# First attention's steps in the order scores, turn, values, turn, and the perceptron's opening units and sums in another order

## The chip, the cores and the metric

The kernel runs on one core of one Trainium2 chip. The metric is device time in microseconds (us), the median of several runs. The core has TensorE for matmuls and transposes, VectorE, ScalarE and GpSimd for the rest, and SyncE, which issues the transfers. Each engine takes its own list of instructions in the order in which the program writes it, and engines meet at semaphores.

## The reference

Two blocks run one after the other on 256 tokens of width 1024, all in float32. What bears on this change is the first layer of the first block:

```
h = h + ab_layer(rms_norm(h, attn_norm[0]))          # two mixers of 8 heads each, then w_out
h = h + square(relu(rms_norm(h, mlp_norm[0]) @ w1)) @ w2   # w1 1024 x 4096, w2 4096 x 1024

fox_mixer, per head:  p = softmax(q k^T / 8 + cum_q - cum_k, causal);   o = p v
dsa_mixer, per head:  p = softmax(latent scores, over the 64 keys picked per query);   o = p v
```

The second layer has another attention (16 heads) and a second perceptron of the same form. The second block, attention again in four steps and a projection, is not touched.

## The kernel before, in words

Weights come as 270 units of 128 x 1024 numbers. ScalarE rounds a unit to its high part (L458), VectorE subtracts to get the low part (L463), and TensorE multiplies high by high, high by low and low by high; this pair of instructions is called a split. The order of everything is written out by hand.

**First attention.** Eight steps, numbered 0 to 7, have two heads each; steps 0 to 3 are the mixer with decay, 4 to 7 the one with picked keys. A step passes through these stages:

- *scores* on TensorE (`ab_scores`, L999, for steps 0 to 3 with L994 before it);
- *peaks* on VectorE (`ab_peaks`, L2000): four passes that add the mask, store the scores in `probs` and find the rows' maxima. `probs` has three slots, so the peaks of a step wait until both turns of the step three before it are through (`s_turned`);
- *exponentials* on ScalarE (L1481), and a reciprocal on GpSimd (L1893);
- two *turns* on TensorE (`turn_p`, L974): three transposes each into the one PSUM bank `ptp`, the first turn for head 0, the second for head 1;
- after each turn a copy out of `ptp`: the first by ScalarE (`p_first`, L1469), the second by VectorE (`p_second`, L2030). A turn waits (`s_copied`) until the copy of the turn before it is done, since the bank is one;
- *values* on TensorE (`mix`, L444): twelve matmuls of 64 columns into `misc`;
- a scaling on VectorE (`ab_scaled`, L2036) into `o_tok`.

Iteration `it` handles the scores and peaks of step `it`, the exponentials of step `it - 1`, the turns and copies of step `it - 3`, and the values and scaling of step `it - 4`. `ab_iter` sets the order on TensorE; a loop at the end of the part for VectorE and one in the part for ScalarE set theirs. In some iterations they also split the first three units of the output projection, and in iterations 8 and 9 blocks of `o_tok` are turned (L408) and copied (L473, L488).

**Perceptron.** `mlp` is called twice, once per layer. Its first two hidden units of 128 need no loop: per unit eight *wide* matmuls (L815, 512 columns: high weights by both parts of x) and eight *narrow* ones (L822, 256 columns: low weights by the high part). The first unit sums in `ptp`, the second in `misc`. Between them stand the turns of the last four column blocks of h (L408), which wait for VectorE's sum into h (L1991). When a unit's narrow ones are done, ScalarE copies half of the bank (`cross`, L1501), VectorE adds it to the other half (`up_sum`, first instruction, L2062) and squares (L2067), ScalarE rounds (`high`, L1507) and VectorE subtracts (`low`, L2072). The wide matmuls of hidden unit 2 use the first bank again and wait for unit 0's L2062; those of unit 3 wait for unit 1's.

Of the kernel before, what the change touches and what calls it, by code (L numbers as in the profile page):

```python
# [60 lines left out]
LEAD = 3  # L61
# [143 lines left out]
def program(nc, x, stream, consts_d, cols_d, rows_d, sel_d, out):  # L205
    with ExitStack() as ctx:  # L206
# [470 lines left out]

        STEPS_AB = A_HEADS // 2 + B_HEADS // 2
        FOX = B_HEADS // 2
        STEPS_C = C_HEADS  # L680
        CO_SPLITS = (5, 8, 14)

# [91 lines left out]
        def _(pe):  # L774
# [25 lines left out]
            def turn_h(b, h0, cc):  # L800

                pe.wait_ge(h_done, h0 + 2 * (cc // 2) + 2)
                pe_turn_block(pe, b, h, (cc,))

            def mlp(f0, u0, b, h0, next_b, next_h0):
                def up_wide(f, u, i=None, blocks_k=range(KD)):

                    if blocks_k[0] == 0:
                        pe.wait_ge(w_lo, at(u + 1, i, UPS))
                    if blocks_k[0] == 0 and f0 + f >= 2:  # L810
                        pe.wait_ge(z_summed, at(f0 + f - 1, i, TPP))
                    for k in blocks_k:
                        if f == 0 and k % 2 == 0:
                            pe.wait_ge(lo_out, 4 * b + k // 2 + 1)
                        nc.tensor.matmul((ptp, misc)[f % 2][:, :], wh[:, u % SPLIT, k * P:(k + 1) * P],  # L815
                                         xhl[:, KD + k, :, :].rearrange("p a s -> p (a s)"),
                                         start=k == 0, stop=False, skip_group_check=True)

                def up_narrow(f, u, blocks_k=range(KD)):

                    for k in blocks_k:
                        last = nc.tensor.matmul((ptp, misc)[f % 2][:, 0:SEQ], wl[:, u % SPLIT, k * P:(k + 1) * P],  # L822
                                                xh[:, KD + k, :], start=False, stop=k == KD - 1,
                                                skip_group_check=True)
                    if blocks_k[-1] == KD - 1:
                        last.then_inc(w_used, 1)

                def down_part(f, u, half, tiles=range(T), opens=False):

                    ws = slice(half * 512, (half + 1) * 512)  # L830
                    for t in tiles:
                        ts = slice(t * P, (t + 1) * P)
                        last = mm3(acc[2 * half + t][:, :], hh[:, f % 2, ts], hl[:, f % 2, ts],
                                   wh[:, u % SPLIT, ws], wl[:, u % SPLIT, ws], opens, f == FT - 1)
                    return last

                def down_ready(f, u, i=None):
                    pe.wait_ge(w_lo, at(u + 1, i, UPS))
                    pe.wait_ge(hid_lo, at(f0 + f + 1, i, TPP))

                def down(f, u, i=None):

                    down_ready(f, u, i)
                    down_part(f, u, 0, opens=f == 0)
                    down_part(f, u, 1, opens=f == 0).then_inc(w_used, 1)

                up_wide(0, u0, blocks_k=range(4))
                turn_h(b, h0, 2)
                turn_h(b, h0, 3)
                up_wide(1, u0 + 1, blocks_k=range(4))  # L850
                up_narrow(0, u0, range(4))
                up_narrow(1, u0 + 1, range(4))
                for ks in (range(4, 6), range(6, KD)):
                    up_wide(0, u0, blocks_k=ks)
                    up_wide(1, u0 + 1, blocks_k=ks)
                up_narrow(0, u0, range(4, KD))
                up_narrow(1, u0 + 1, range(4, KD))

                def two_tiles(f, i=None):

                    u = u0 + 2 + 2 * f
                    up_wide(f + 2, u, i)
                    up_wide(f + 3, u + 1, i)
                    up_narrow(f + 2, u)
                    up_narrow(f + 3, u + 1)
                    down(f, u + 2, i)
                    down(f + 1, u + 3, i)

                for f in range(0, TPP, 2):
                    two_tiles(f)  # L870
                with pe.Fori(0, PASSES - 1) as i:
                    for f in range(TPP, 2 * TPP, 2):
                        two_tiles(f, i)
                u = u0 + 2 * FT - 2
                down_ready(FT - 2, u)
                down_part(FT - 2, u, 0)
                down_ready(FT - 1, u + 1)
                down_part(FT - 1, u + 1, 0).then_inc(half_summed, 1)
                down_part(FT - 2, u, 1).then_inc(w_used, 1)
                down_part(FT - 1, u + 1, 1, (0,))  # L880
                turn_h(next_b, next_h0, 0)
                down_part(FT - 1, u + 1, 1, (1,)).then_inc(w_used, 1)
                turn_h(next_b, next_h0, 1)
# [126 lines left out]

            def ab_iter(it):

                if 0 <= it - DEEP < STEPS_AB:
                    turn_p(it - DEEP, 0)
                if it < STEPS_AB:
                    ab_scores(it)
                if it >= STEPS_AB:
                    mix(it - DEEP - 1, ab_values(it - DEEP - 1))
                if 0 <= it - DEEP < STEPS_AB:
                    turn_p(it - DEEP, 1)  # L1020
                if DEEP < it < STEPS_AB:
                    if it == DEEP + 1:
                        pe.wait_ge(ev_act, left(G_ABO))
                        pe.wait_ge(ev_dve, left(G_ABO))
                    mix(it - DEEP - 1, ab_values(it - DEEP - 1))

            def between(u):

# [422 lines left out]
        def _(act):  # L1451
# [43 lines left out]
            def mlp(f0, u0, n, next_b, next_gain):  # L1495
                def cross(f, u_end, i=None):

                    act.wait_ge(w_used, at(u_end, i, UPS))
                    if f0 + f >= 2:
                        act.wait_ge(z_summed, at(f0 + f - 1, i, TPP))  # L1500
                    s_.activation(probs[:, f % 2, 0:SEQ], (ptp, misc)[f % 2][:, SEQ:2 * SEQ],  # L1501
                                  ACT.Copy).then_inc(z_cross, 1)

                def high(f, u_free, i=None):
                    act.wait_ge(sqr_done, at(f0 + f + 1, i, TPP))
                    act.wait_ge(w_used, at(u_free, i, UPS))
                    s_.activation(hh[:, f % 2, :], hq[:, f % 2, :], ACT.Copy).then_inc(hid_hi, 1)  # L1507

                split(u0 + LEAD)
                cross(0, u0 + 1)  # L1510
                split(u0 + 1 + LEAD)
                cross(1, u0 + 2)
                high(0, u0)
                high(1, u0)
                act_sumsq(act, n)
                with act.Fori(0, PASSES) as i:
                    for f in range(0, TPP, 2):
                        u = u0 + 2 + 2 * f
                        split(u + LEAD, i)
                        cross(f + 2, u + 1, i)  # L1520
                        split(u + 1 + LEAD, i)
                        cross(f + 3, u + 2, i)
                        split(u + 2 + LEAD, i)
                        high(f + 2, u + 3, i)
                        split(u + 3 + LEAD, i)
                        high(f + 3, u + 4, i)
                u = u0 + 2 * FT - 2
                split(u + LEAD)
                act_turn_block(act, next_b, next_gain, (0, 1))
                split(u + 1 + LEAD)  # L1530
# [91 lines left out]
            for it in range(1, STEPS_AB + DEEP):  # L1622
                if 0 <= it - DEEP < STEPS_AB:
                    p_first(it - DEEP)
                if it - 1 < STEPS_AB:
                    exponentials(it - 1)
                if 0 <= it - (STEPS_AB - 3) < LEAD:
                    split(U_ABO + it - (STEPS_AB - 3))
                if it in (STEPS_AB, STEPS_AB + 1):
                    act_turn_block(act, 1, ccs=(it - STEPS_AB,))  # L1630
                if it == 1:
# [338 lines left out]
        def _(dve):  # L1970
# [84 lines left out]
            def mlp(f0, u0, next_b, next_gain):  # L2055
# [18 lines left out]

                split(u0 + LEAD)
                up_sum(0)
                split(u0 + 1 + LEAD)
                low(0)
                up_sum(1)
                low(1)  # L2080
                with dve.Fori(0, PASSES) as i:
                    for f in range(0, TPP, 2):
# [150 lines left out]
                scaled(st, o_tok[:, :, 2 * HD * st:2 * HD * (st + 1)].rearrange("p t (a d) -> p a t d", a=2), rs)  # L2233

            for it in range(STEPS_AB + DEEP):
                if 0 <= it - DEEP < STEPS_AB:
                    p_second(it - DEEP)
                if it < STEPS_AB - 1:
                    ab_peaks(it)
                if it > DEEP:  # L2240
                    ab_scaled(it - DEEP - 1)
                if it == STEPS_AB - 1:
                    ab_peaks(it)
                if 0 <= it - (STEPS_AB - 2) < LEAD:
                    split(U_ABO + it - (STEPS_AB - 2))
                if it in (STEPS_AB, STEPS_AB + 1):
                    dve_turn_block(dve, 1, ccs=(it - STEPS_AB,))
                if it == 0:
# [445 lines left out]
```

## Time and profile before

| what | value |
|---|---|
| median of 3 runs | 907.81 us (907.81 to 908.78) |
| the profiled execution, its own time | 908.62 us |
| its span, first to last instruction | 906.8 us |
| TensorE busy | 890.7 us, 98% of the span |
| VectorE busy | 645.2 us |
| ScalarE busy | 510.1 us |
| mean granted TensorE clock | 0.998 |
| first attention's last turn begins | 115.85 us |

A share near 98% says that time is lost only where TensorE stands still or runs at a lower clock, so the places where it waits are read one by one in its timeline. In a timeline row the first number is the start, the second the duration; square brackets hold the idle time before it and the engine that ended it. Durations of TensorE's instructions overlap, so distances between starts are the better measure.

### The profile page before, as it was taken

How to read it: one execution, taken by the hardware profiler on the slowest of the kernel's cores; microseconds unless marked ns; L12 is line 12 of the kernel's file. 1: busy time of each engine (PE TensorE's matmuls, PEld its weight loads, DVE VectorE, ACT ScalarE, POOL GpSimd, SP SyncE). 2: the span in 40 equal slices, each digit the busy share in tenths (PEclk: the TensorE clock that was granted, in tenths of full speed). 3: DMA queues.
4: the chain of work that ended last, by engine and by line, in shares of the span. 5: the costliest groups of instructions: out<-in, count | busy, mean ns of one | idle time of the engine just before them, and what ended most of it. 6: DMA issues, size and time to landing. Idle time of an engine off the chain costs nothing. (4 is left out here: it accounts for less than half of the span.)

```text
span 906.8 us, 14857 instructions
## 1 busy us (share of the span) xinstructions
PE 890.7 (98%) x4796; PEld 745.2 (82%) x4796; DVE 645.2 (71%) x1305; ACT 510.1 (56%) x1017; POOL 124.5 (14%) x168
## 2 busy tenths in 40 slices
PE   8999999999999999999999999999999999999998
PEld 7878787888888888888878888888887778878876
DVE  4768756766666679687467666666876878777775
ACT  6654835444454466586354454444656666666573
POOL 1310300000000000354010000000430401400401
PEclk9999999999999999999999999999999999999999
DMA  9643143655555557010436565555464445454431
GB/s 343 225 158 98 46 144 123 210 198 191 191 194 193 190 178 247 33 47 25 140 116 217 196 192 192 195 191 188 141 223 145 140 140 182 147 182 141 162 117 47
DMA packets 41609, 145.75 MB, mean 161 GB/s; under 512 B 4688, under 2 KB 6224, under 8 KB 41552
## 3 DMA queue, kind: packets, MB, share of 16 engines
q1 hardware_dynamic: 41264, 144.93, 48.4%
q8 instruction: 34, 0.56, 0.3%
q14 instruction: 23, 0.19, 0.1%
q10 hardware_dynamic: 288, 0.07, 0.0%
HBM read 143.93 MB, written 1.05 MB: 160 GB/s over the span
## 5 line engine op out<-in xcount | busy, mean ns | idle before, releaser
L463 DVE TENSOR_TENSOR wl<-raw,wh 128x1024 fp32r<-128x1024 f32 (+2 forms) x270 | 329.1, 1222 | 88.7 <-ACT wh L458 86.2
L458 ACT ACTIVATE wh<-raw 128x1024 fp32r<-128x1024 f32 (+2 forms) x270 | 281.6, 1046 | 64.9 <-PE acc L355 43.4
L353 PE MATMUL acc<-wh,xhl 128*128 128x512 f32 (+1 forms) x472 | 190.7, 404 | 0.6 <-DVE xhl L2490 0.4
L355 PE MATMUL acc<-wh,xhl 128*128 128x512 f32 (+1 forms) x472 | 184.4, 391 | 0.0
L354 PE MATMUL acc<-wl,xhl 128*128 128x512 f32 (+1 forms) x472 | 183.9, 390 | 0.0
L353 PEld LDWEIGHTS acc<-wh,xhl 128*128 128x128 f32 x472 | 88.7, 188 | 25.0 <-issue 8.0
L355 PEld LDWEIGHTS acc<-wh,xhl 128*128 128x128 f32 x472 | 88.6, 188 | 19.2
L354 PEld LDWEIGHTS acc<-wl,xhl 128*128 128x128 f32 x472 | 88.8, 188 | 16.3
L353 PE MATMUL acc<-wh,hh 128*128 128x512 f32 x256 | 100.2, 391 | 0.0
L354 PE MATMUL acc<-wl,hh 128*128 128x512 f32 x256 | 100.0, 391 | 0.0
L355 PE MATMUL acc<-wh,hl 128*128 128x512 f32 x256 | 99.6, 389 | 0.0
L1507 ACT ACTIVATE hh<-hq 128x256 fp32r<-128x256 f32 x64 | 26.7, 418 | 77.3 <-PE acc L355 72.5
L815 PE MATMUL ptp<-xhl,wh 128*128 128x512 f32 x256 | 64.1, 390 | 1.1 <-DVE hr L2062 1.1
L1501 ACT ACTIVATE probs<-ptp 128x256 f32<-128x256 f32 x32 | 12.3, 383 | 93.7 <-PE ptp L822 93.7
L815 PE MATMUL misc<-xhl,wh 128*128 128x512 f32 x256 | 64.3, 391 | 0.7 <-DVE hr L2062 0.7
L2062 DVE TENSOR_TENSOR hr<-ptp,probs 128x256 f32<-128x256 f32 x32 | 13.6, 424 | 67.5 <-ACT probs L1501 67.5
L507 POOL TENSOR_SCALAR st<-st 128x2 f32<-128x2 f32 x7 | 2.4, 338 | 430.8 <-ACT o_tok L500 258.2
L815 PEld LDWEIGHTS misc<-xhl,wh 128*128 128x128 f32 x256 | 47.8, 188 | 11.2 <-DVE wl L463 1.5
L815 PEld LDWEIGHTS ptp<-xhl,wh 128*128 128x128 f32 x256 | 47.8, 188 | 11.2 <-issue 1.4
L355 PEld LDWEIGHTS acc<-wh,hl 128*128 128x128 f32 x256 | 48.1, 188 | 10.2
L353 PEld LDWEIGHTS acc<-wh,hh 128*128 128x128 f32 x256 | 48.2, 188 | 9.3
L354 PEld LDWEIGHTS acc<-wl,hh 128*128 128x128 f32 x256 | 48.2, 188 | 8.7
(302 smaller groups left out, 1355.2 us busy)
## 6 DMA issues: line engine op xcount, KB each, us to landing
raw<-stream SPq DMA_DIRECT2D x266, 512.0 KB, 3.4
raw<-stream SPq DMA_DIRECT2D x4, 352.0 KB, 5.7
h<-x SPq DMA_DIRECT2D x4, 256.0 KB, 4.0
out<-h SPq DMA_DIRECT2D x3, 256.0 KB, 2.1
row<-rows SPq DMA_DIRECT2D x1, 700.0 KB, 8.8
probs<-sel SPq DMA_DIRECT2D x1, 512.0 KB, 7.7
cst<-consts SPq DMA_DIRECT2D x1, 507.0 KB, 7.1
out<-h SPq DMA_DIRECT2D x2, 128.0 KB, 2.0
```

Of the source, the lines that this page charges most:

```text
L353: nc.tensor.matmul(out_, ah, bh, start=start, stop=False, skip_group_check=True)
L354: nc.tensor.matmul(out_, ah, bl, start=False, stop=False, skip_group_check=True)
L355: return nc.tensor.matmul(out_, al, bh, start=False, stop=stop_, skip_group_check=True)
L458: nc.scalar.activation(used(u, wh[:, u % SPLIT, :]), used(u, raw[:, u % RAW, :]), ACT.Copy).then_inc(w_hi, 1)
L463: nc.vector.tensor_tensor(used(u, wl[:, u % SPLIT, :]), used(u, raw[:, u % RAW, :]), used(u, wh[:, u % SPLIT, :]).bitcast(F32), ALU.subtra ...
L507: chain_link(nc.gpsimd.tensor_scalar(dst, src, 1.0 / width, EPS, ALU.mult, ALU.add))
L815: nc.tensor.matmul((ptp, misc)[f % 2][:, :], wh[:, u % SPLIT, k * P:(k + 1) * P], xhl[:, KD + k, :, :].rearrange("p a s -> p (a s)"), star ...
L1501: s_.activation(probs[:, f % 2, 0:SEQ], (ptp, misc)[f % 2][:, SEQ:2 * SEQ], ACT.Copy).then_inc(z_cross, 1)
L1507: s_.activation(hh[:, f % 2, :], hq[:, f % 2, :], ACT.Copy).then_inc(hid_hi, 1)
L2062: v_.tensor_tensor(hr[:, f % 2, :], bank[:, 0:SEQ], probs[:, f % 2, 0:SEQ], ALU.add).then_inc(z_summed, 1)
```

## The change

It has four parts.

1. TensorE, first attention: iterations 4 to 7 issue scores, first turn, values, second turn. Before, they issued first turn, scores, second turn, values.
2. VectorE, first attention: an iteration issues peaks, scaling, copy of the second turn. Before: copy, peaks, scaling (in iteration 7 copy, scaling, peaks).
3. The three splits of the output projection's units stand in iterations 3, 4 and 6 on ScalarE and 4, 5 and 7 on VectorE. Before: 5, 6, 7 and 6, 7, 8.
4. Perceptron, both calls: the narrow matmuls of unit 0 stand earlier in both halves of the opening, and ScalarE and VectorE do both copies and both sums ahead of the second split.

```diff
+        ABO_SPLITS = (3, 4, 6)
...
                 up_wide(0, u0, blocks_k=range(4))
+                up_narrow(0, u0, range(4))
                 turn_h(b, h0, 2)
                 turn_h(b, h0, 3)
                 up_wide(1, u0 + 1, blocks_k=range(4))
-                up_narrow(0, u0, range(4))
                 up_narrow(1, u0 + 1, range(4))
-                for ks in (range(4, 6), range(6, KD)):
-                    up_wide(0, u0, blocks_k=ks)
-                    up_wide(1, u0 + 1, blocks_k=ks)
+                up_wide(0, u0, blocks_k=range(4, 6))
+                up_wide(1, u0 + 1, blocks_k=range(4, 6))
+                up_wide(0, u0, blocks_k=range(6, KD))
                 up_narrow(0, u0, range(4, KD))
+                up_wide(1, u0 + 1, blocks_k=range(6, KD))
                 up_narrow(1, u0 + 1, range(4, KD))
...
             def ab_iter(it):
-                if 0 <= it - DEEP < STEPS_AB:
-                    turn_p(it - DEEP, 0)
+                if it == DEEP:
+                    turn_p(0, 0)
                 if it < STEPS_AB:
                     ab_scores(it)
-                if it >= STEPS_AB:
+                if DEEP < it < STEPS_AB + DEEP:
+                    turn_p(it - DEEP, 0)
+                if it == DEEP + 1:
+                    pe.wait_ge(ev_act, left(G_ABO))
+                    pe.wait_ge(ev_dve, left(G_ABO))
+                if it > DEEP:
                     mix(it - DEEP - 1, ab_values(it - DEEP - 1))
                 if 0 <= it - DEEP < STEPS_AB:
                     turn_p(it - DEEP, 1)
-                if DEEP < it < STEPS_AB:
-                    if it == DEEP + 1:
-                        pe.wait_ge(ev_act, left(G_ABO))
-                        pe.wait_ge(ev_dve, left(G_ABO))
-                    mix(it - DEEP - 1, ab_values(it - DEEP - 1))
...
ScalarE, mlp
                 split(u0 + LEAD)
                 cross(0, u0 + 1)
+                cross(1, u0 + 2)
                 split(u0 + 1 + LEAD)
-                cross(1, u0 + 2)
                 high(0, u0)
                 high(1, u0)
...
ScalarE, first attention
-                if 0 <= it - (STEPS_AB - 3) < LEAD:
-                    split(U_ABO + it - (STEPS_AB - 3))
+                if it in ABO_SPLITS:
+                    split(U_ABO + ABO_SPLITS.index(it))
...
VectorE, mlp
                 split(u0 + LEAD)
                 up_sum(0)
+                up_sum(1)
                 split(u0 + 1 + LEAD)
                 low(0)
-                up_sum(1)
                 low(1)
...
VectorE, first attention
             for it in range(STEPS_AB + DEEP):
-                if 0 <= it - DEEP < STEPS_AB:
-                    p_second(it - DEEP)
-                if it < STEPS_AB - 1:
+                if it < STEPS_AB:
                     ab_peaks(it)
                 if it > DEEP:
                     ab_scaled(it - DEEP - 1)
-                if it == STEPS_AB - 1:
-                    ab_peaks(it)
-                if 0 <= it - (STEPS_AB - 2) < LEAD:
-                    split(U_ABO + it - (STEPS_AB - 2))
+                if 0 <= it - DEEP < STEPS_AB:
+                    p_second(it - DEEP)
+                if it - 1 in ABO_SPLITS:
+                    split(U_ABO + ABO_SPLITS.index(it - 1))
```

What stands in a row on VectorE in iteration 5 (the second turn's copy of step 2, the peaks of step 5, the scaling of step 1), each row with the semaphores it waits for. Iteration 4 has the same form but another mask. Before:

```order
L2030 COPY pt<-ptp 128x384 [waits s_mixed,s_turned]
L2000 ISA probs,nb<-pair,picked 128x128 [waits s_scored,s_turned]
L2000 ISA nb 128x1
L2000 ISA probs,nb<-pair,picked 128x256
L2000 ISA nb 128x1
L2000 ISA probs,nb<-acc,picked 128x128 [waits s_scored]
L2000 ISA nb 128x1
L2000 ISA probs,nb<-acc,picked 128x256
L2000 ISA nb 128x1
L2036 TENSOR_TENSOR o_tok<-misc,rs 128x2x2x64 [waits s_coef,s_mixed]
```

After (two or three lines further down in the file):

```order
L2003 ISA probs,nb<-pair,picked 128x128 [waits s_scored,s_turned]
L2003 ISA nb 128x1
L2003 ISA probs,nb<-pair,picked 128x256
L2003 ISA nb 128x1
L2003 ISA probs,nb<-acc,picked 128x128 [waits s_scored]
L2003 ISA nb 128x1
L2003 ISA probs,nb<-acc,picked 128x256
L2003 ISA nb 128x1
L2039 TENSOR_TENSOR o_tok<-misc,rs 128x2x2x64 [waits s_coef,s_mixed]
L2033 COPY pt<-ptp 128x384 [waits s_mixed,s_turned]
```

The copy moved from ahead of the four passes and the scaling to behind them; the passes wait for the same `s_turned` count as the copy.

TensorE from the second turn of step 0 on (L974 a turn, L999 the scores of step 4, L444 the values of step 0). Before:

```order
L974 MATMUL ptp<-cst,probs 128x128 [waits s_copied,s_exped]
L974 MATMUL ptp<-cst,probs 128x128 x2
L974 MATMUL ptp<-cst,probs 128x128 [waits s_copied,s_exped]
L974 MATMUL ptp<-cst,probs 128x128 x2
L999 MATMUL pair<-QK 128x128 [waits s_peaked]
L999 MATMUL acc<-QK 128x128
L999 MATMUL pair<-QK 128x256
L999 MATMUL acc<-QK 128x256
L974 MATMUL ptp<-cst,probs 128x128 [waits s_copied,s_exped]
L974 MATMUL ptp<-cst,probs 128x128 x2
L444 MATMUL misc<-Y,pt 128x64 [waits s_copied,ev_dve,ev_act]
L444 MATMUL misc<-Y,pt 128x64 x5
```

After:

```order
L977 MATMUL ptp<-cst,probs 128x128 [waits s_copied,s_exped]
L977 MATMUL ptp<-cst,probs 128x128 x2
L1002 MATMUL pair<-QK 128x128 [waits s_peaked]
L1002 MATMUL acc<-QK 128x128
L1002 MATMUL pair<-QK 128x256
L1002 MATMUL acc<-QK 128x256
L977 MATMUL ptp<-cst,probs 128x128 [waits s_copied,s_exped]
L977 MATMUL ptp<-cst,probs 128x128 x2
L444 MATMUL misc<-Y,pt 128x64 [waits s_copied,ev_dve,ev_act]
L444 MATMUL misc<-Y,pt 128x64 x5
L977 MATMUL ptp<-cst,probs 128x128 [waits s_copied,s_exped]
L977 MATMUL ptp<-cst,probs 128x128 x2
```

The first turn of step 1 moved behind the scores, its second turn behind the values of step 0.

TensorE in the perceptron's opening, from the last column blocks' turns on (`ptp` holds hidden unit 0, `misc` unit 1). Before:

```order
L408 MATMUL pair<-cst,h 128x128 x3
L815 MATMUL misc<-xhl,wh 128x512 [waits w_lo]
L815 MATMUL misc<-xhl,wh 128x512 x3
L822 MATMUL ptp<-xhl,wl 128x256 x4
L822 MATMUL misc<-xhl,wl 128x256 x4
L815 MATMUL ptp<-xhl,wh 128x512 [waits lo_out]
L815 MATMUL ptp<-xhl,wh 128x512
L815 MATMUL misc<-xhl,wh 128x512 x2
L815 MATMUL ptp<-xhl,wh 128x512 [waits lo_out]
L815 MATMUL ptp<-xhl,wh 128x512
L815 MATMUL misc<-xhl,wh 128x512 x2
L822 MATMUL ptp<-xhl,wl 128x256 x4
```

After:

```order
L408 MATMUL pair<-cst,h 128x128 x3
L816 MATMUL misc<-xhl,wh 128x512 [waits w_lo]
L816 MATMUL misc<-xhl,wh 128x512 x3
L823 MATMUL misc<-xhl,wl 128x256 x4
L816 MATMUL ptp<-xhl,wh 128x512 [waits lo_out]
L816 MATMUL ptp<-xhl,wh 128x512
L816 MATMUL misc<-xhl,wh 128x512 x2
L816 MATMUL ptp<-xhl,wh 128x512 [waits lo_out]
L816 MATMUL ptp<-xhl,wh 128x512
L823 MATMUL ptp<-xhl,wl 128x256 x4
L816 MATMUL misc<-xhl,wh 128x512 x2
L823 MATMUL misc<-xhl,wl 128x256 x4
```

Four narrow matmuls of unit 0 left this stretch (they now stand ahead of the turns of h), and its last four stand ahead of unit 1's last two wide ones.

## Rows read from the trace of the kernel before

**Rows 1.** The page: busy time of each engine, and the granted clock in 40 slices.
```profile
PE 890.7 (98%) x4796; PEld 745.2 (82%) x4796; DVE 645.2 (71%) x1305; ACT 510.1 (56%) x1017; POOL 124.5 (14%) x168
...
PEclk9999999999999999999999999999999999999999
```

**Rows 2.** Timeline of TensorE, first attention: start, duration, what, idle before.
```profile
94.53 0.55 PE L974 MATMUL ptp<-cst,probs 128*128 128x128 f32 x3
95.82 0.52 PE L974 MATMUL ptp<-cst,probs 128*128 128x128 f32 x3 [0.74 <-DVE pt L2030]
...
97.12 0.55 PE L974 MATMUL ptp<-cst,probs 128*128 128x128 f32 x3
97.51 1.45 PE L444 MATMUL misc<-Y,pt 128*128 128x64 f32 x12
98.79 0.50 PE L974 MATMUL ptp<-cst,probs 128*128 128x128 f32 x3
...
107.75 0.50 PE L974 MATMUL ptp<-cst,probs 128*128 128x128 f32 x3
...
111.23 0.52 PE L974 MATMUL ptp<-cst,probs 128*128 128x128 f32 x3 [0.41 <-DVE pt L2030]
...
114.16 0.52 PE L974 MATMUL ptp<-cst,probs 128*128 128x128 f32 x3 [0.30 <-DVE pt L2030]
...
115.85 0.50 PE L974 MATMUL ptp<-cst,probs 128*128 128x128 f32 x3
```

**Rows 3.** Timeline of VectorE, first attention.
```profile
95.11 0.56 DVE L2030 COPY pt<-ptp 128x384 f32<-128x384 f32 x1 [0.61 <-PE ptp L974]
...
104.09 0.28 DVE L2000 CUSTOM_DVE_ANT_0 probs<-pair,picked 128x128 f32<-128x128 f32 x1
...
105.19 0.42 DVE L2036 TENSOR_TENSOR o_tok<-misc,rs 128x256 f32<-128x256 f32 x1
105.53 1.22 DVE L463 TENSOR_TENSOR wl<-raw,wh 128x1024 fp32r<-128x1024 f32 x1
```

**Rows 4.** Timeline of TensorE, perceptron's opening and first loop units.
```profile
142.95 1.09 PE L408 MATMUL pair<-cst,h 128*128 128x128 f32 x8 [0.66 <-DVE h L1991]
...
147.60 0.64 PE L822 MATMUL ptp<-xhl,wl 128*128 128x256 f32 x4
148.07 0.64 PE L822 MATMUL misc<-xhl,wl 128*128 128x256 f32 x4
149.26 2.09 PE L815 MATMUL ptp<-xhl,wh 128*128 128x512 f32 x8 [0.55 <-DVE hr L2062]
151.68 2.08 PE L815 MATMUL misc<-xhl,wh 128*128 128x512 f32 x8 [0.32 <-DVE hr L2062]
...
160.98 1.98 PE L815 MATMUL ptp<-xhl,wh 128*128 128x512 f32 x8
162.79 1.98 PE L815 MATMUL misc<-xhl,wh 128*128 128x512 f32 x8
```

**Rows 5.** Timelines of ScalarE (first row) and VectorE, perceptron's opening.
```profile
148.28 0.39 ACT L1501 ACTIVATE probs<-ptp 128x256 f32<-128x256 f32 x1 [2.11 <-PE ptp L822]
...
144.52 1.66 DVE L491 SCALAR_TENSOR_TENSOR xhl<-pair,col,xhl 128x256 fp32r<-128x256 f32 x4 [1.62 <-ACT xhl L476]
...
148.69 0.42 DVE L2062 TENSOR_TENSOR hr<-ptp,probs 128x256 f32<-128x256 f32 x1 [1.10 <-ACT probs L1501]
...
151.12 0.42 DVE L2062 TENSOR_TENSOR hr<-misc,probs 128x256 f32<-128x256 f32 x1
```

**Rows 6.** Second attention: stretches (us, busy by engine, clock, DMA), and TensorE rows.
```profile
375.70:379.10 3.40, 2.02 (x16) 1.59 (x15) 2.78 (x18) 2.69 (x12) 2.84 (x7) 1.00 0.02 5
379.10:382.50 3.40, 3.40 (x17) 3.10 (x15) 0.09 (x1) 2.01 (x8) 2.06 (x4) 0.50 0.00 0
...
381.54 0.84 PE L974 MATMUL ptp<-cst,probs 128*128 128x128 f32 x3
382.17 1.62 PE L444 MATMUL misc<-Y,pt 128*128 128x64 f32 x12
```

## The prediction, made before the changed kernel was run

> **What bounds the kernel now.** I read the page's busy line first: TensorE is busy 98% of the span and the granted clock stands at 9 tenths or more in all 40 slices [rows 1]. So the time is TensorE's, and an edit counts by what it does to TensorE's gaps and clock. Then I read TensorE's timeline for gaps where the change acts. In the first attention they are small: 0.74, 0.41 and 0.30 us before turns [rows 2]. In the perceptron's opening there are 0.66 us before the turns of h and then two waits for VectorE's sum [rows 4]. Last I read VectorE's timeline between the turns, since part 2 of the change reorders it [rows 3].
>
> **Part by part: the first attention.** The bank `ptp` is one, so four events form a chain: second turn, VectorE's copy, next first turn, ScalarE's copy, next second turn. The edit on TensorE alone is neutral: the same instructions stand in the same cycle, and only what covers which copy changes. From turn over scores to turn takes 97.12 - 95.82 = 1.30 us, turn to values 97.51 - 97.12 = 0.39, values to turn 98.79 - 97.51 = 1.28 [rows 2]; the sum of 2.97 is the step's pace when nothing waits. VectorE's copy begins 95.11 - 94.53 = 0.58 us after its turn begins, and the next turn 95.82 - 95.11 = 0.71 after that [rows 2, 3]: 1.29 us, which the 1.30 of the scores would just cover.
>
> But VectorE now does peaks and scaling before that copy. The peaks cannot be done early: they reuse the `probs` slot of the step three before, and so wait for the same second turn as the copy. All of it falls between second turn and next first turn. The peaks take 105.19 - 104.09 = 1.10 us and the scaling 105.53 - 105.19 = 0.34 [rows 3]. From second to next first turn it is then 0.58 + 1.10 + 0.34 + 0.71 = 2.73 us where TensorE has 1.30 of work, 1.43 idle per step; the step's pace becomes 2.73 + 0.39 + 1.28 = 4.40.
>
> In times of this trace: the second turn of step 0 stays at 94.53. The first turn of step 1 follows after 0.58 + 1.10 + 0.71 = 2.39 (nothing to scale yet), at 96.92 where it was 95.82. The first turns of steps 2 to 5 follow at a pace of 4.40 (0.39 + 1.28 + 2.73): 101.32, 105.72, 110.12, 114.52. That of step 5 was at 107.75 [rows 2], so it is 6.77 late. It still waits for the peaks of step 7, with no scores left to fill, so that gap is the widest: 2.73 less some 0.4 of the turn itself, 2.3 us. From there no peaks are left, and a step is as the last one was before, 114.16 - 111.23 = 2.93, and the last two turns 115.85 - 114.16 = 1.69 apart [rows 2]: 114.52 + 2 x 2.93 + 1.69 = 122.07 for the last turn instead of 115.85. **First attention: +6.2 us.** That sum has the gain in it that the splits, moved out of iteration 8, no longer hold back the copy of step 5.
>
> The moved splits: on VectorE each is 1.22 us [rows 3] behind the copy in iterations 4, 5 and 7, where VectorE next waits for a second turn 1.67 us (0.39 + 1.28) after the first turn that this copy released; that hides it. On ScalarE they stand behind exponentials that are not needed for over a step. Cost nothing; if the cover failed, at most 1.2 us once. SyncE reloads the raw slots some us sooner; nobody waits for these.
>
> **The clock.** In the second attention TensorE was busy 2.02 us of 3.40, in small matmuls, and in the next 3.40 us the granted clock was 0.50, the lower of its two levels, 1.2 GHz [rows 6]. In the new first attention TensorE will be busy 2.97 us of 4.40, and just before the first turn of step 5 it stands still for 2.3 us. I expect such a fall at least there. Its price: a turn followed by values took 382.17 - 381.54 = 0.63 us at the lower level, and 0.39 at full clock [rows 2, 6], a factor of 1.6. Over a fall as long as that one it loses 3.4 x (1 - 1/1.6) = 1.3 us if TensorE is on the path throughout, nothing if it lies in a gap. I take one, **+1.3 us**; the ends are 0 and four such falls, 5.2, one for every second step or so of the stretch from 96 to 122.
>
> Here a page speaks against me. The Trainium skill, in "TensorE: Matmul & The Clock Gate", section "Why this matters for your kernels", says to allow no idle gaps over some 3 us or the clock is halved; by it none of these gaps would matter and the clock term is 0. This case's trace does not agree: the fall in rows 6 followed gaps that together are only 1.4 us. So I keep the term, and the rule as a rival.
>
> **The perceptron's opening, twice.** Four narrow matmuls of unit 0 (148.07 - 147.60 = 0.47 us) move into the gap of 0.66 before the turns of h, whose end VectorE's sum sets [rows 4]. What follows moves up by 0.47 at most. It must still wait for VectorE's low parts, which come from 144.52 on over 1.66 us [rows 5]; by their halves that limits the shift to about 0.3. Second, unit 0's narrow ones end two wide matmuls sooner. At 1.81 us per eight wide ones (162.79 - 160.98) [rows 4] two take 0.46. So its last narrow ones start at 147.60 - 0.3 - 0.46 = 146.84. The sum starts 148.69 - 147.60 = 1.09 after them and the wide ones of unit 2 149.26 - 148.69 = 0.57 after that [rows 4, 5]: at 148.50, 0.76 sooner. Third, unit 3: its wait is for the sum of unit 1, at 151.12 behind the split and the low part of unit 0 [rows 5]. Now it stands ahead of both: unit 1's narrow ones at 147.77, sum 148.86, ready 149.43. TensorE reaches unit 3 at 148.50 + 1.81 = 150.31. It was 151.68, so 1.37 sooner; I take 1.3, since the low parts may hold back a little more. Bounds: 0 and the whole lag, 151.68 - 148.07 - 0.47 - 1.81 = 1.33 of waits, plus the 0.47, so 1.8. The delayed split is needed only by the down matmuls, some 3.7 us later. The second perceptron has the same instructions: **2 x -1.3 = -2.6 us**. The loop behind it shows no gap whose end is set by ScalarE or VectorE, so the gain stays.
>
> **Sum.** +6.2 + 1.3 - 2.6 = +4.9 us. The profiled execution took 908.62 with a span of 906.8; it would become 913.5. The median of the runs is 907.81, 0.8 below it, so the median becomes 912.7.
>
> **Rivals.**
> - *The clock does not fall* (the page's rule above): +6.2 - 2.6 = +3.6, 911.4. For it: a gap of 0.74 and one of 0.66 alone left no mark in the clock [rows 2, 4]. Against it: rows 6. Chance 0.25.
> - *The clock falls three or four times*: 3.9 to 5.2 in place of 1.3, 915.3 to 916.6. For it: every step from 4 to 8 has such a gap. Against: at the lower clock TensorE fills more of its gap. 0.13.
> - *The perceptron gives nothing* because the sums wait for something else or the loop gives it back: 915.3. The loop's even pace speaks against it. 0.08.
> - *Half of the stall*: the stage has slack that I overlook and a step costs 0.7, not 1.43: attention about +3, total 908.2 without and 909.5 with a fall of the clock. 0.05.
> - *Faster, the other side*: the copy is not really held back, because the peaks are ready before the second turn. Then VectorE's copy is covered by the scores (1.29 against 1.30), ScalarE's by the values, the gaps of 0.74, 0.41 and 0.30 go, and with the perceptron -4, 903.8. It decides at one point: whether the peaks wait for `s_turned`. Their row in the new order has that wait, so only 0.03. The same holds for the change not doing what it says.
>
> **How the numbers follow.** My forecast, one fall of the clock or two partly hidden, holds 0.46. About 0.2% (1.8 us) can be told from no change by a measurement of this kernel. Slower by more than that, above 909.6, are the forecast and the first three rivals: 0.92. Same, the fourth: 0.05. Faster: 0.03. The range reaches from the no-fall case with a smaller stall, 909.8, to repeated falls, 916.5.
>
> **What the new profile would show.** VectorE's copy (L2033) about 1.4 us later behind its turn than before, in four steps, with TensorE idle 1.1 us once, about 1.4 three times, and over 2 before the first turn of step 5; the last turn near 122 us, or 123.5 with a fall of the clock. The granted clock at 0.5 for some us between 100 and 120. In each perceptron the wide matmuls of unit 3 start 1.3 us closer to the end of the turns of h, with no wait. I am wrong if the pace of steps 4 to 7 stays at 3.0, if the clock stays at 1.00, or if the perceptron's start has another wait as long as the old.

## The result

The changed kernel takes 917.69 us (median of 6 runs, 915.19 to 919.82) against 908.13 for the kernel before (6 runs, 907.81 to 909.59): a ratio of 1.0104, with a 95% interval of 1.009 to 1.0118. It is slower, as forecast, but by 9.6 us and not by 4.9, and lies above the range. The profiled execution took 916.45 with a span of 914.6; before it was 908.62 and 906.8.

The page of the changed kernel: busy time of each engine and granted clock, to be read against [rows 1].

```profile
PE 894.6 (98%) x4796; PEld 749.8 (82%) x4796; DVE 645.9 (71%) x1305; ACT 510.5 (56%) x1017; POOL 124.4 (14%) x168
...
PEclk9999979999999999999999999999999999999999
```

The sixth slice (114 to 137 us) has fallen to 7 tenths. TensorE's busy time *rose* by 3.9 us with the same 4796 matmuls: at the lower clock they take longer. So busy time is no measure of work here.

TensorE in the first attention of the changed kernel (start, duration, what, idle before), the rows that answer to [rows 2]:

```profile
95.03 0.55 PE L977 MATMUL ptp<-cst,probs 128*128 128x128 f32 x3
...
97.43 0.52 PE L977 MATMUL ptp<-cst,probs 128*128 128x128 f32 x3 [1.00 <-DVE pt L2033]
97.78 1.45 PE L444 MATMUL misc<-Y,pt 128*128 128x64 f32 x12
...
101.75 0.52 PE L977 MATMUL ptp<-cst,probs 128*128 128x128 f32 x3 [1.33 <-DVE pt L2033]
...
103.40 0.50 PE L977 MATMUL ptp<-cst,probs 128*128 128x128 f32 x3
...
106.08 0.52 PE L977 MATMUL ptp<-cst,probs 128*128 128x128 f32 x3 [1.33 <-DVE pt L2033]
...
110.41 0.52 PE L977 MATMUL ptp<-cst,probs 128*128 128x128 f32 x3 [1.33 <-DVE pt L2033]
...
114.73 0.66 PE L977 MATMUL ptp<-cst,probs 128*128 128x128 f32 x3 [2.18 <-DVE pt L2033]
115.18 2.66 PE L444 MATMUL misc<-va,pt 128*128 128x64 f32 x12
117.64 0.85 PE L977 MATMUL ptp<-cst,probs 128*128 128x128 f32 x3
...
126.18 0.50 PE L977 MATMUL ptp<-cst,probs 128*128 128x128 f32 x3
```

There are the five gaps of the forecast, each ended by VectorE's copy: 1.00, three of 1.33, 2.18, 7.2 us in all. The pace, from one step's first turn to the next step's, is 106.08 - 101.75 = 4.33 us. From 114.73 on there is hardly a gap, yet twelve matmuls of 64 columns take 2.66 us where they took 1.45. From the second turn of step 0 to the last turn it is 126.18 - 95.03 = 31.15 us, against 115.85 - 94.53 = 21.32 [rows 2]: 9.83 more.

VectorE inside one such gap of the changed kernel, to be read against [rows 3]; the turn before it is at 103.40 and the one it releases at 106.08.

```profile
103.93 0.29 DVE L2003 CUSTOM_DVE_ANT_0 probs<-pair,picked 128x128 f32<-128x128 f32 x1 [1.19 <-PE ptp L977]
...
105.05 0.42 DVE L2039 TENSOR_TENSOR o_tok<-misc,rs 128x256 f32<-128x256 f32 x1
105.39 0.55 DVE L2033 COPY pt<-ptp 128x384 f32<-128x384 f32 x1
105.85 1.22 DVE L463 TENSOR_TENSOR wl<-raw,wh 128x1024 fp32r<-128x1024 f32 x1
```

VectorE had been idle for 1.19 us, waiting for the second turn (103.40). It then does peaks for 1.12 us, the scaling for 0.34 and only then the copy. 0.53 + 1.12 + 0.34 + 0.69 = 2.68 from turn to turn, where 2.73 was forecast.

The clock, in three stretches of the changed kernel (length, busy time and number of instructions of TensorE, its weight loads, VectorE, ScalarE and GpSimd, then granted clock, DMA share, GB/s):

```profile
94.53:115.00 20.47, 13.31 (x118) 10.61 (x115) 12.82 (x56) 13.75 (x48) 5.96 (x6) 1.00 0.15 52
115.00:125.20 10.20, 10.20 (x51) 9.68 (x49) 3.87 (x7) 4.28 (x13) 1.01 (x1) 0.50 0.15 53
125.20:130.00 4.80, 4.80 (x33) 4.31 (x32) 2.23 (x4) 1.55 (x3) 0.00 (x0) 1.00 0.11 21
```

The whole stretch with the gaps runs at full clock, with TensorE busy 13.31 of 20.47 us. Then the clock is at its lower level, 1.2 GHz, for 10.2 us in which TensorE is busy all the time. That is one execution; another one of the same attention has its low time elsewhere (see the attention alone).

TensorE in the perceptron's opening of the changed kernel, the rows that answer to [rows 4]:

```profile
152.43 0.63 PE L823 MATMUL ptp<-xhl,wl 128*128 128x256 f32 x4
153.25 1.09 PE L408 MATMUL pair<-cst,h 128*128 128x128 f32 x8 [0.19 <-DVE h L1994]
...
157.23 0.64 PE L823 MATMUL ptp<-xhl,wl 128*128 128x256 f32 x4
...
158.18 0.62 PE L823 MATMUL misc<-xhl,wl 128*128 128x256 f32 x4
158.90 2.09 PE L816 MATMUL ptp<-xhl,wh 128*128 128x512 f32 x8
160.82 1.99 PE L816 MATMUL misc<-xhl,wh 128*128 128x512 f32 x8
```

The gap of 0.66 is down to 0.19 and both waits for `hr` are gone. From the last turn of the attention to unit 3's wide matmuls it is 160.82 - 126.18 = 34.64, against 151.68 - 115.85 = 35.83: 1.19 less. In the second perceptron, from the first wide matmuls of the opening to those of unit 3, it is 475.06 - 465.75 = 9.31, against 467.13 - 456.66 = 10.47: 1.16 less.

### The profile page after: what moved, and what is told of

It is laid out like the page before. It is cut to its first block and busy times, and to the rows that moved or that the text cites. A ratio compares the mean times of both kernels' runs of the same rounds, so it can differ in the third digit from the quotient of the medians.

```text
span 914.6 us, 14857 instructions
## 1 busy us (share of the span) xinstructions
PE 894.6 (98%) x4796; PEld 749.8 (82%) x4796; DVE 645.9 (71%) x1305; ACT 510.5 (56%) x1017; POOL 124.4 (14%) x168
## 5 line engine op out<-in xcount | busy, mean ns | idle before, releaser
L2065 DVE TENSOR_TENSOR hr<-ptp,probs 128x256 f32<-128x256 f32 x32 | 13.6, 424 | 66.9 <-ACT probs L1504 66.9
L355 PEld LDWEIGHTS acc<-wh,hl 128*128 128x128 f32 x256 | 48.1, 188 | 10.2
```

The costliest lines, as they stand in the source:

```text
L355: return nc.tensor.matmul(out_, al, bh, start=False, stop=stop_, skip_group_check=True)
L2065: v_.tensor_tensor(hr[:, f % 2, :], bank[:, 0:SEQ], probs[:, f % 2, 0:SEQ], ALU.add).then_inc(z_summed, 1)
```

## The experiments

Ratios are to the kernel before, run beside on the same chip, with 95% intervals. "Turns" are from the second turn of step 0 to the last turn: 21.32 us before, 31.15 after. Diffs are against the changed kernel unless it says otherwise.

### The attention alone, the perceptron alone

The first keeps the changed attention and puts the perceptron's opening (`up_narrow`, `up_wide`, `cross`, `up_sum`) back; the second is the other half.

```diff
-                up_narrow(0, u0, range(4))
...
-                up_wide(0, u0, blocks_k=range(4, 6))
-                up_wide(1, u0 + 1, blocks_k=range(4, 6))
-                up_wide(0, u0, blocks_k=range(6, KD))
+                for ks in (range(4, 6), range(6, KD)):
+                    up_wide(0, u0, blocks_k=ks)
+                    up_wide(1, u0 + 1, blocks_k=ks)
```

> Parts 1 to 3 of the change, with the perceptron's opening as before. Theory (the attention loses, the perceptron gains, and the two add up): the last turn of the first attention is 9 to 11 us later than the 115.85 of before, the perceptron's opening is as before, and the time is the changed kernel's plus 2.4, about 920. Rival (the perceptron's new order costs part of the loss, through the weights' splits that it delays): the time is below the changed kernel's 917.7.

Measured: 917.58 (915.76 to 917.79), ratio 1.0094 [1.0078, 1.0109]. The turns take 31.67 with the same gaps (1.00, 1.33 three times, 2.18), and both waits for `hr` are back. It was to be 2.4 slower than the changed kernel and has the same median. The gain of the perceptron can't be read from this pair of medians: the clock's low time differs between runs of one kernel by more than that (the changed kernel's six runs go from 915.19 at a mean granted clock of 0.994 to 919.82 at 0.987). The traces do show it: from the last turn to unit 3's wide matmuls it is 162.33 - 126.53 = 35.80 here, against 34.64. Two stretches of this kernel:

```profile
94.86:112.00 17.14, 12.16 (x108) 10.00 (x107) 9.93 (x41) 12.25 (x43) 4.46 (x5) 1.00 0.18 62
112.00:125.60 13.60, 11.42 (x55) 10.52 (x54) 6.41 (x17) 5.44 (x20) 2.02 (x2) 0.50 0.12 40
```

Here the clock fell at 112.0, ahead of the gap of 2.18 (its turn begins at 114.78), and stayed low for 13.6 us. So in the same attention the fall came once behind the widest gap and once before it.

> Part 4 of the change alone, the attention as before. Theory: the wide matmuls of hidden unit 3 start 34.64 us after the attention's last turn where it was 35.83, 1.2 us sooner in each of two perceptrons, and nothing gives it back: the median is 2.4 below the 908.1 of before, 905.7. Rival (the loop behind the opening gives it back): within 0.5 of before.

Measured: 905.01 (904.41 to 906.18), ratio 0.9965 [0.9952, 0.9979], turns 21.33. Its row of unit 3:

```profile
150.67 1.98 PE L815 MATMUL misc<-xhl,wh 128*128 128x512 f32 x8
```

It stands 34.69 us after the last turn at 115.98; before it was 35.83. In the second perceptron it is 463.48 - 454.17 = 9.31 from the opening's first wide matmuls, where before it was 10.47. So each perceptron gives 1.14 to 1.19 us, and part 4 alone makes the kernel faster. Its span is 3.7 us shorter than before's. The two perceptrons give 2.3 of that, and this execution had no fall of the clock in the second attention, which is worth about 1.6 (see "The clock in the kernel before").

### The copy first

VectorE does scaling, copy, peaks, in place of peaks, scaling, copy; all other parts of the change stay.

```diff
-                if it < STEPS_AB:
-                    ab_peaks(it)
                 if 0 <= it - DEEP < STEPS_AB:
                     p_second(it - DEEP)
+                if it < STEPS_AB:
+                    ab_peaks(it)
```

> The changed kernel with VectorE's order in the first attention set to scaling, copy of the second turn, peaks; TensorE's order, the splits and the perceptron stay changed. Theory (the stall is the copy queued behind the peaks on VectorE, and the clock's fall follows from the stall): the gaps of 1.33 us go, the pace of steps 1 to 4 is 2.97, the clock stays at 1.00, the last turn comes at about 115.4 after a start as before's, and the median is 905 to 905.5. Rival 1 (TensorE's new order costs by itself, whoever copies): gaps of some 1 us stay and the time stays above 912. Rival 2 (the clock falls through the moved splits or by chance): the gaps go but the clock still falls, 908 to 910.

Measured: 905.08 (904.36 to 906.09), ratio 0.9963 [0.995, 0.9977]; turns 20.82. TensorE of this kernel:

```profile
98.93 0.38 PE L1002 MATMUL acc<-QK 64*128 64x256 f32 x1
99.24 0.55 PE L977 MATMUL ptp<-cst,probs 128*128 128x128 f32 x3
99.62 1.45 PE L444 MATMUL misc<-Y,pt 128*128 128x64 f32 x12
```

The first turn (99.24) follows the last scores (98.93) with no gap, and the twelve values follow it. So the whole loss hangs on where the peaks stand among VectorE's calls: the same TensorE order is 0.5 us *quicker* than before's once the copy stands first. That also shows the prediction's estimate that the scores just cover the copy.

### A fourth slot for the peaks

The peaks keep their place ahead of the copy, but write to a fourth slot (three free columns of `QK` as the fourth), so they need the turns of four steps back.

```diff
-                pb = probs[:, st % DEEP, :]
+                pb = slot(st)
...
-                if st >= DEEP:
-                    dve.wait_ge(s_turned, 2 * (st - DEEP + 1))
+                if st > DEEP:
+                    dve.wait_ge(s_turned, 2 * (st - DEEP))
```

> The changed kernel with a fourth slot for the first attention's probabilities (steps 3 and 7 use columns of QK that are free then), so that the peaks of a step wait for the turns of the step four before it, not three. The orders of all engines stay as changed. Theory (the copy is late only because the peaks ahead of it wait for the same turn's count, through the slot that they reuse): the peaks start about 1 us after their scores, the copy 0.58 after its turn, the gaps of 1.33 us go, the clock stays, and the median is 904.5 to 905.5. Rival (the three instructions ahead of the copy delay it whenever they start): gaps near 1 us stay, 912 or more.

Measured: 905.58 (904.55 to 906.18), ratio 0.9961 [0.9946, 0.9976]. TensorE:

```profile
94.67 0.55 PE L985 MATMUL ptp<-cst,probs 128*128 128x128 f32 x3
...
96.58 0.52 PE L985 MATMUL ptp<-cst,probs 128*128 128x128 f32 x3 [0.51 <-DVE pt L2041]
...
99.51 0.55 PE L985 MATMUL ptp<-cst,probs 128*128 128x128 f32 x3
...
102.50 0.52 PE L985 MATMUL ptp<-cst,QK 128*128 128x128 f32 x3
```

One gap of 0.51 is left at step 1, and the pace is 102.50 - 99.51 = 2.99. So it is not VectorE's order alone that costs, but the order together with the wait for the slot: the peaks ahead of the copy can't start before the turn that the copy waits for. Either one taken away ends the stall. In the traces of both kernels the clock is at 1.00 all through the first attention, so its fall there came with the stall.

### TensorE's new order alone

Part 1 of the change alone. Against before:

```diff
-                if 0 <= it - DEEP < STEPS_AB:
-                    turn_p(it - DEEP, 0)
+                if it == DEEP:
+                    turn_p(0, 0)
...
+                if DEEP < it < STEPS_AB + DEEP:
+                    turn_p(it - DEEP, 0)
```

> Part 1 alone: TensorE's new order in the first attention, everything else as before. Theory (the chain worked out from the traces): the copy is now in time, but the scaling stands behind the peaks and the values of steps 1, 2 and 3 wait for it, about 1.0 us each; the last turn comes near 118.5, 2.6 later than before, and the median is 910.5 to 911.5, more if the clock falls. Rival (TensorE's order is neutral by itself, as the prediction said): within 0.5 of before.

Measured: 912.05 (910.07 to 915.29), ratio 1.0044 [1.0027, 1.0061]; turns 24.02. TensorE and, in the second fence, VectorE of this kernel:

```profile
98.89 0.55 PE L974 MATMUL ptp<-cst,probs 128*128 128x128 f32 x3
100.29 1.52 PE L444 MATMUL misc<-Y,pt 128*128 128x64 f32 x12 [0.85 <-DVE o_tok L2036]
101.65 0.50 PE L974 MATMUL ptp<-cst,probs 128*128 128x128 f32 x3
```

```profile
98.15 0.56 DVE L2030 COPY pt<-ptp 128x384 f32<-128x384 f32 x1 [1.29 <-PE ptp L974]
98.62 0.28 DVE L2000 CUSTOM_DVE_ANT_0 probs<-pair,picked 128x128 f32<-128x128 f32 x1
...
99.73 0.42 DVE L2036 TENSOR_TENSOR o_tok<-misc,rs 128x256 f32<-128x256 f32 x1
```

The turn no longer waits, but the values do: they reuse `misc`, which the scaling must have read, and the scaling stands behind peaks that start 0.47 after the copy. Three gaps of 0.85. The prediction called TensorE's edit neutral by itself; it isn't. The wait moves to the next instruction held by VectorE's queue. Both waits go with VectorE's order scaling, copy, peaks, or with the fourth slot. The median is 3.1 above before, though the turns take 2.70 more. Five of the nine runs have a mean granted clock of 0.998 or 1.000 (910.07 to 912.05) and four have 0.994 (913.85 to 915.29); where the clock was low in those four isn't known (of the 21 runs of before beside them, two have 0.992 and take 912.4 and 912.5).

### The gaps filled

Matmuls of zeros, 512 columns each, by a helper that the kernel has: 5 in each 1.33 gap, 8 in the widest. The stall is meant to stay and only TensorE's idling to go.

```diff
+                if DEEP + 2 <= it <= STEPS_AB:
+                    keep_clock(acc[3], 5 if it < STEPS_AB else 8)
```

> The changed kernel with matmuls of zeros (128x512, into a bank that nobody reads then) put ahead of the first turns that wait: five in iterations 5, 6 and 7, eight in iteration 8. They lie in the gaps, so the stall stays and only TensorE's activity changes. Theory (of the 9.6 us lost, 6 are the stall, -2.4 the perceptron, and the remaining 6 the lower clock): the clock stays at 1.00 through the first attention, the pace stays 4.33, and the median is 911.5 to 912.5 with a spread of under 2 us. Rival (the lower clock costs little because it lies in the gaps, and the stall is worth more than the one trace shows): above 915.

Measured: 912.34 (910.89 to 912.78), ratio 1.0041 [1.0028, 1.0055]. A filler, the first turn of step 5 and the last turn; then the whole stretch:

```profile
104.59 1.43 PE L789 MATMUL acc<-zero 128*128 128x512 f32 x5
...
114.64 0.52 PE L977 MATMUL ptp<-cst,probs 128*128 128x128 f32 x3 [0.33 <-DVE pt L2035]
...
122.04 0.50 PE L977 MATMUL ptp<-cst,probs 128*128 128x128 f32 x3
```

```profile
94.93:122.30 27.37, 25.43 (x195) 20.78 (x193) 16.29 (x59) 18.41 (x61) 6.46 (x7) 1.00 0.17 59
```

The fillers delay nothing: the first turn of step 5 comes 114.64 - 94.93 = 19.71 after the second of step 0, where it was 19.70 without them. The turns take 122.04 - 94.93 = 27.11 us at full clock, so the stall alone is 27.11 - 21.32 = 5.79. The rest of the changed kernel's 9.83, 4.04 us, is the clock, and all of it lies behind the first turn of step 5 (126.18 - 114.73 = 11.45, against 122.04 - 114.64 = 7.40). In medians the clock's share is 917.69 - 912.34 = 5.35.

### Which gap brings the clock down

The same filler in the three 1.33 gaps only (`if DEEP + 2 <= it < STEPS_AB: keep_clock(acc[3], 5)`), then in the widest only (`if it == STEPS_AB: keep_clock(acc[3], 8)`).

> The changed kernel with five matmuls of zeros in each gap of 1.33 us (iterations 5 to 7) and none in the widest gap, ahead of the first turn of step 5. Theory (the widest gap, 2.2 us, is enough for the clock to fall, whatever comes before): the clock falls in the first attention as it does in the changed kernel, and the median is 914 to 918. Rival (it is the sum of the gaps over the steps that matters): the clock stays, 911.5 to 912.5.

Measured: 914.25 (911.96 to 916.86), ratio 1.0062 [1.0042, 1.0082].

```profile
94.92:116.20 21.28, 18.10 (x139) 14.33 (x138) 13.06 (x52) 14.29 (x51) 5.46 (x6) 1.00 0.15 50
116.20:119.60 3.40, 3.40 (x18) 3.14 (x17) 1.67 (x3) 2.30 (x8) 1.01 (x1) 0.50 0.43 159
```

> The changed kernel with eight matmuls of zeros in the widest gap and none in the gaps of 1.33 us. Theory (the widest gap starts the fall): the clock stays in the first attention in most runs, 911.5 to 913. Rival (the gaps of 1.33 us, one per 4.33, are enough): the clock falls, 914 to 918.

Measured: 913.24 (910.88 to 920.58), ratio 1.0051 [1.0026, 1.0076].

```profile
95.16:108.00 12.84, 9.19 (x82) 7.57 (x81) 7.93 (x31) 9.08 (x33) 3.45 (x4) 1.00 0.12 41
108.00:118.20 10.20, 9.60 (x40) 7.70 (x38) 5.13 (x21) 4.18 (x16) 2.01 (x2) 0.50 0.14 52
...
114.34 3.76 PE L789 MATMUL acc<-zero 128*128 128x512 f32 x8
```

With the steps filled the clock falls at 116.2, behind the gap of 2.18, and is low for 3.4 us. That execution was the shortest of the six; the others have a mean granted clock of 0.992 to 0.997 and go up to 916.86. With the widest gap filled the clock falls at 108.0, before that gap and after one gap of 1.00 and two of 1.33, and stays low for 10.2 us. So neither kind of gap is needed and neither is harmless; the attention alone, where nothing was filled, agrees, with its fall at 112.0. The second kernel has a cost of its own: at the lower clock its eight fillers take 3.76 us (2.10 in the kernel with all gaps filled, at full clock) and hold up the turn behind them, which comes 117.90 - 113.84 = 4.06 after the turn before it and not 2.68. Its runs lie far apart: the shortest, 910.88, had a granted clock of 1.000 over the span, the longest, 920.58, of 0.985. What decides in one run where the clock falls, and for how long, is not settled; filling both kinds of gap is what removed the loss.

### The clock in the kernel before

Before plus three zero matmuls in the second attention's iteration 3, where [rows 6] has its fall.

```diff
+                    keep_clock(acc[3], 3)
```

> The kernel before, with three matmuls of zeros in the second attention's iteration 3, in the gap of 0.66 us ahead of the turn of the queries. The runs of the kernel before stand in two groups, near 907.5 with a mean clock of 1.000 and near 909.1 with 0.998. Theory (the groups are one fall of the clock in the second attention, 3.4 us at the lower level, which costs 1.6, and half of the idle time removed is enough to avoid it): most runs near 907.5, the trace without a stretch at 0.50. Rival (the fall does not hang on that gap): the same two groups.

Measured: 907.63 (906.81 to 908.03, 11 runs) against 908.91 (907.25 to 912.11, 21 runs), ratio 0.9983 [0.9972, 0.9993]. The filler and the two stretches of [rows 6] in this kernel:

```profile
378.59 0.94 PE L788 MATMUL acc<-zero 128*128 128x512 f32 x3
```

```profile
375.70:379.10 3.40, 2.69 (x19) 2.24 (x19) 2.88 (x17) 3.21 (x15) 2.31 (x6) 1.00 0.02 5
379.10:382.50 3.40, 3.40 (x27) 2.71 (x25) 1.29 (x8) 2.06 (x9) 2.61 (x5) 1.00 0.00 0
```

The fall is gone, and all 11 runs have a mean granted clock of 0.999 or 1.000. Before's own 21 runs stand in groups: about 907.4 with a granted clock of 1.000, 909.0 with 0.998, and two at 912 with 0.994. So one fall of 3.4 us costs about 909.0 - 907.4 = 1.6 us.

> The kernel with VectorE's order scaling, copy, peaks and all else as changed, plus the same three matmuls of zeros in the second attention. Theory: the runs without a fall of the clock gave 904.4 to 905.1 for that order; with the second attention's fall avoided the median is 904.4 to 904.9. Rival (the fall comes anyway, or from another gap): 905 to 906.

The kernel with the copy first and this filler: 904.55 (904.37 to 905.32), ratio 0.9951 [0.9934, 0.9969]. It has the lowest median of all and is faster than both the kernel before and the changed one.

### The moved splits

Parts 3 and 4 with before's orders in the attention.

```diff
-                if 0 <= it - (STEPS_AB - 3) < LEAD:
-                    split(U_ABO + it - (STEPS_AB - 3))
+                if it in ABO_SPLITS:
+                    split(U_ABO + ABO_SPLITS.index(it))
```

> Parts 3 and 4, with both orders of the first attention as before. Theory: moving the splits only takes them out of the way of two copies, so the last turn comes 0.3 to 0.6 sooner (near 115.4) and the median is 904.3 to 904.9, against 905.0 for part 4 alone. Rival (the moved splits cost, on ScalarE ahead of a copy): the last turn is later and the median above 905.5.

Measured: 905.94 (905.32 to 907.17), ratio 0.9971 [0.9961, 0.9981]; turns 21.66, 0.34 more than before, where 0.3 to 0.6 less was expected: the rival holds. ScalarE and then TensorE of this kernel:

```profile
96.46 1.04 ACT L458 ACTIVATE wh<-raw 128x1024 fp32r<-128x1024 f32 x1
97.41 0.47 ACT L1472 ACTIVATE pt<-ptp 128x384 f32<-128x384 f32 x1
```

```profile
96.38 0.52 PE L977 MATMUL ptp<-cst,probs 128*128 128x128 f32 x3 [0.74 <-DVE pt L2033]
98.02 0.52 PE L977 MATMUL ptp<-cst,probs 128*128 128x128 f32 x3 [0.27 <-ACT pt L1472]
```

ScalarE now splits just before its copy, which starts 97.41 - 96.38 = 1.03 after its turn, where it was 0.55 before. In before's order this holds up TensorE. In the changed kernel the turn comes later (97.43) than this split ends (96.40 + 1.04), the copy starts 0.55 after it, and the split is hidden. The gaps of 0.42 and 0.31 in the last steps stayed though the split had left iteration 8, so it wasn't the splits that held back those turns. From the first turn of step 5 to that of step 6 it is 112.13 - 108.65 = 3.48, as before.

## Why the prediction was right in sign and short in size

- **The stall, +6.2.** Right: 5.79 by the filled kernel. This is not luck: the gaps came in the forecast places, 1.00, 1.33 three times and 2.18 against 1.1, 1.4 and 2.3, the pace 4.33 against 4.40. The first turn of step 5 came 114.73 - 95.03 = 19.70 after the second of step 0, against 114.52 - 94.53 = 19.99. The cause, peaks that wait for the same turn as the copy behind them, is shown from two sides: by the copy first and by the fourth slot.
- **"TensorE's edit alone is neutral."** Wrong, though the sum didn't rest on it: alone it costs three waits of 0.85.
- **The splits, nothing.** Right in the changed kernel, whose gaps are all VectorE's copy; by themselves they cost 0.34. The gain for step 5 that the sum counts on came, but not from them: from its first turn to that of step 6 it was 111.23 - 107.75 = 3.48 before, is 117.52 - 114.64 = 2.88 in the filled kernel, where the sum had 2.93, and stays 3.48 with the splits moved alone. TensorE's order alone gives 114.01 - 110.97 = 3.04.
- **The perceptron, -2.6.** Right: 1.19 + 1.16 = 2.35 in the changed kernel's trace, 1.14 + 1.16 = 2.30 with part 4 alone.
- **The clock, +1.3: the step that failed.** "I take one" fall of 3.4 us. The profiled execution had 10.2 us at the lower level in the first attention and lost 4.04 by it; in medians it is 5.35, just past the far end of 0 to 5.2. That the clock would fall was right. What was mis-sized is the length: the sum took one fall as long as the one that the trace before happened to show, with no reason why the clock should be back after it. It stayed low while turns and 64-column values kept TensorE busy, for 10.2 us here and 13.6 in the attention-only kernel. The sum's other assumption, that no gap hides the loss, held in the profiled execution, where the low time lay behind the last stall. The price per us was about right: 4.04 in 10.2 is 0.40, against 1.3 in 3.4, which is 0.38. What sets the length, and why it differs between executions of one kernel, stays open.
- The sum by measured terms is 5.79 + 4.04 - 2.35 = +7.48. The stretch began 95.03 - 94.53 = 0.50 later than before, ahead of any edit; together 7.98, and the spans differ by 7.8 (both executions had one fall of 3.4 us in the second attention, at about 379 and 388). In medians it is 5.79 + 5.35 - 2.35 = 8.79 of the 9.56 measured; no run shows where the other 0.8 went.
- **The rule weighed against it.** The Trainium skill, "TensorE: Matmul & The Clock Gate", "Why this matters for your kernels", has gaps of over some 3 us as what halves the clock. The traces do not agree: the longest gap here was 2.18, and the clock fell; with these gaps filled and the pace the same it stayed at 1.00. The rival built on the rule named 911.4.

The rival of three or four falls named 915.3 to 916.6, nearest to the 917.69 that came, and had 0.13. The six runs of the changed kernel alone lie 919.82 - 915.19 = 4.6 us apart, so a range that ended at 916.5 was also too narrow at the top.

## What to carry to other kernels

Before moving an instruction in an in-order queue, write down what *each* instruction ahead of it waits for: if one waits for the same event, as here through a reused slot, the move puts its whole duration on the path, and either another order or one more slot ends that. A stall that repeats every few us on a TensorE-bound kernel costs more than its gaps, because the clock may fall and then stays low while the engine is busy again; price it by filling the gaps with matmuls of zeros, which splits stall from clock in one run. Fill all the gaps: where the clock fell all the same, eight fillers took 3.76 us in place of 2.10 and became a delay themselves. And taking a wait off one instruction is a gain only if the next instruction that waits for the same engine does not take it over, as the values did when TensorE's order changed alone.

## What the runs showed of the hardware

- The granted clock stayed at its lower level for 10.2 us in which TensorE was busy 10.20, with transposes and 64-column matmuls; the next wide matmuls start at 126.44, behind it. In other executions it was low for 3.4 us (the kernel before, in its second attention, and the changed one with the gaps of 1.33 filled), for 10.2 (with the widest gap filled) and for 13.6 (the attention alone).
- Low time varies between executions of one kernel: the mean granted clock of the changed kernel was 0.987 to 0.994, its times 915.19 to 919.82.
- Gaps of 1.33 us at a pace of 4.33, with none longer before it, were enough for a fall in two executions (at 108.0 and 112.0); with these gaps filled by 1.4 us of zero matmuls and the widest by 2.10, the clock stayed at 1.00.
- Three zero matmuls (0.94 us) in a pause of the second attention are worth 0.17% of the kernel before.
- From one engine to the other and back: VectorE's first operation begins 0.53 us after the turn that releases it begins (103.40, 103.93), and the next turn 0.69 after the copy begins (105.39, 106.08).
